# Picking both sides' indices of a head in three VectorE steps of 512 columns in place of six of 256, with the row buffers moved to the front of the memory

## The chip, the core and the metric

The kernel runs on one core of a Trainium2 chip. The metric is the device time of one launch in microseconds (us), lower is better. TensorE (PE) multiplies matrices, VectorE (DVE) and ScalarE (ACT) work on 128 partitions at a time, GpSimd (POOL) issues the indirect gathers, SyncE (SP) the plain loads. The engines run beside each other and meet at semaphores; each takes its own instructions in the order of the program.

## What is computed

Two layers of a decoder trunk on 256 tokens of width 1024. Each layer has a mixing part (norm, one input projection, pooling and attention, output projection) and a feed-forward part that looks up experts by product keys:

```
q = (xc @ w_q).reshape(TOKEN_CHUNK, PEER_HEADS, 2, PEER_HALF)
s = einsum('thpd,pkd->thpk', q, sub_keys)           # 8 heads, 2 sides, 128 keys
sv, si = top_k(s, 16)                               # per head and side
cand = sv[:, :, 0, :, None] + sv[:, :, 1, None, :]  # 16 x 16 sums
cand_id = si[:, :, 0, :, None] * 128 + si[:, :, 1, None, :]
cv, ci = top_k(cand.reshape(..., 256), 16)
eid = take_along_axis(cand_id.reshape(..., 256), ci)
g = softmax(cv)
y = einsum('thk,thkd->td', g * gelu(einsum('thkd,td->thk', u[eid], xc)), v[eid])
```

So every token reads 8 x 16 = 128 rows of `u` and of `v` per layer, from tables of 16384 rows of 1024 float32. That is the bulk of what the kernel moves.

## The kernel before

**Windows and ticks.** The tokens are cut into two tiles of 128, a token per partition, and a window is one tile in one layer: `windows` = 4, in the order layer 0 tile 0, layer 0 tile 1, layer 1 tile 0, layer 1 tile 1. A window has 64 ticks of two expert rows each, 128 rows in all. A row is one gather by POOL (L1365): for each of the 128 tokens one line of `uv`, u and v side by side, 8 KB per partition and 1 MB in all, into one of seven buffers of `ring`. The last four rows are gathered in halves (L1371, L1376).

**A row's way.** VectorE's `dot` (L1201) multiplies the u half with the token, 1024 columns, and adds it up. ScalarE makes the row's weight of it (L887 to L895). Then the v half is added to the token in one of two ways: either ScalarE spreads the weight over a diagonal (L905) and TensorE multiplies diagonal and row into the two `ybank` sums (L686, four instructions a row), or VectorE adds it itself (`weighted`, L1214). `rows_on_tensor` says which: in ticks that lie in the set `shared`, row 0 goes to VectorE, otherwise both go to TensorE. When the sum has taken a row, its buffer is free and POOL gathers the row seven places on.

**The mix of the next window** and its picking run between the rows. `streamed` walks over all ticks, and on each engine it issues the rows of a tick and whatever of the mix generators (`vector_mix`, `tensor_mix`, `scalar_mix`) has come due; each `yield` in those names the tick at which the next piece is due. So every engine's order is fixed, and a piece of mix on VectorE stands between two dots. `first_heads`, `later_heads` and `last_heads` give the ticks of the eight heads' three stages.

**The picking of a head** on VectorE, in `vector_mix`: `key_search` finds the 16 best keys of each side (`sv` their scores, `si` their indices), `all_sums` forms the 256 sums, `sum_search` finds the 16 best (`cv`, and `ci` their places), `places` splits a place into its two indices `cabf` (side 0 and side 1). `pick_side(a, lo, n, hot)` then looks up `si` at these for one side, in three steps, each of which waits for the one before (`settle`): L981 compares the index with 0 to 15 and so writes a one-hot table, L984 multiplies it with the side's key indices `sif`, L987 adds up each line of it into `picked`. For 16 experts the table has 16 x 16 = 256 columns; it is laid over the head's `score`, which is no longer wanted. `experts` (L992, L1000) makes the expert's number of the two, for which POOL waits (`expert_ready`), and `weigh_heads` (L1029, L1031) finishes the softmax. In the general case side 0 is picked half a tick before side 1, so that one dot lies between them.

Head 0 of the first window is taken in two parts, since nothing can be gathered before it: `first_experts` publishes the very best expert (L1015), then seven more from the 8 x 8 best sums, with `pick_side` on 64 columns; eight more follow behind the first dot, with 128 columns.

**Start of the rows.** The gathers of rows 3 to 6 use ring buffers that held weights of window 1 until then; POOL waits until `next_keys_values` on TensorE (L495, L505) has read them.

**Loads.** SP loads the weights in chunks of 1 MB: the first into `ring` buffers, twelve into `held`, all others into the two slots of `wring`.

Of the kernel before, what the change touches and what calls it, by code (L numbers as in the profile page):

```python
# [13 lines left out]
P = 128  # L14
S = 256
NT = S // P
D = 1024
# [116 lines left out]
def build(nc, consts, chunks, uv, x, side, rows, w_pool, pool_scale, out):  # L134
# [3 lines left out]
    with ExitStack() as ctx:  # L138
# [15 lines left out]
        first_gainT = cst[:, C_GAIN:C_DIST].rearrange("p (n k) -> p n k", n=2)  # L154
        later_gainT = beside[:, KEYS:].rearrange("p (n k) -> p n k", n=2)
        wpool = sb("wpool", [P, NG, GOUT])
        held = sb("held", [P, HELD, CHUNK])
        wring = sb("wring", [P, W_SLOTS, CHUNK])
        carry = sb("carry", [P, NG * REACH])
# [18 lines left out]
        cv = sb("cv", [P, TOPK])  # L178
        ci = sb("ci", [P, TOPK], U32)
        cab = sb("cab", [P, 2, TOPK], U32)  # L180
        best = sb("best", [P, 2])
        cabf = sb("cabf", [P, 2, TOPK])
        picked = sb("picked", [P, 2, TOPK])
        cmax = sb("cmax", [P, 1])
# [1 line left out]
        prob = sb("prob", [P, HK])  # L186
        expert = sb("expert", [P, HK], U32)

        last_halves = sb("last_halves", [P, 2, HALVED], U32)
        half_ssq = sb("half_ssq", [P, 1])  # L190

        buf1 = sb("buf1", [P, 2 * D])
        gates = buf1[:, :]
# [7 lines left out]
        merged = buf2[:, D:2 * D]  # L201
        mergedT = merged.rearrange("p (k n) -> p k n", n=P)

        ring = sb("ring", [P, RING, 2 * D])

        next_hT_made = ring[:, 0, D:2 * D].rearrange("p (k n) -> p k n", n=P)
        next_hT = buf1[:, D:2 * D].rearrange("p (k n) -> p k n", n=P)
        dots = sb("dots", [P, COLS])
        half_p = sb("half_p", [P, COLS])
        sq = sb("sq", [P, 2])  # L210
# [698 lines left out]
        def step(ins):  # L909
            ins.then_inc(dve_step, 1)  # L910
            steps[0] += 1
# [11 lines left out]
        def vector_mix(dve, w):  # L923
# [49 lines left out]
                    maximum()  # L973
                    places(TOPK, 4)

            def pick_side(a, lo, n, hot):


                best = hot.shape[2]
                these = slice(lo, lo + n)  # L980
                step(dve.tensor_tensor(hot, cabf[:, a, these].unsqueeze(2).to_broadcast([P, n, best]),  # L981
                                       iota16[:, 0:best].unsqueeze(1).to_broadcast([P, n, best]), ALU.is_equal))
                settle(dve)
                step(dve.tensor_tensor(hot, hot, sif[:, a, 0:best].unsqueeze(1).to_broadcast([P, n, best]),  # L984
                                       ALU.mult))
                settle(dve)
                step(dve.tensor_reduce(picked[:, a, these], hot, AX.X, ALU.add))  # L987
                settle(dve)

            def experts(h, lo, n):  # L990
# [9 lines left out]
                dve.tensor_scalar(expert[:, h * TOPK + lo:h * TOPK + lo + n], picked[:, 0, these],  # L1000
                                  float(layer * EXPERTS), None, ALU.add).then_inc(expert_ready, 1)

            def one_hot(h):
                return score[:, 2 * h:2 * h + 2, :].rearrange("p a (k i) -> p (a k) i", i=TOPK)

            def first_experts():


                for r in range(2):
                    dve.wait_ge(*read(w, f"score0{'ab'[r]}"))  # L1010
                    key_search(0, (r,))

                step(dve.tensor_copy(best[:, :], si[:, :, 0]))
                settle(dve)
                dve.scalar_tensor_tensor(out=expert[:, 0:1], in0=best[:, 0:1], scalar=float(NK),  # L1015
                                         in1=best[:, 1:2], op0=ALU.mult, op1=ALU.add).then_inc(expert_ready, 1)
                sums = tmp[:, 0:64]
                square = sums.rearrange("p (i j) -> p i j", i=8)
                all_sums(square, 8)
                search(lambda r: cv[:, :], lambda r: ci[:, :], lambda r: sums, range(1), (0,))  # L1020
                places(8, 3)
                for a in range(2):
                    pick_side(a, 0, 8, square)
                experts(0, 1, 7)

            def weigh_heads(h):
# [123 lines left out]
            if w == 0:  # L1150
                yield head_tick(w, 0, 0)
                first_experts()
                key_search(0, eights=(8,))
                yield head_tick(w, 0, 1)
                sum_search(0, 0)
                sum_search(0, 8)
                weigh_heads(0)
                yield head_tick(w, 0, 2)
                for a in range(2):
                    pick_side(a, 8, 8, tmp[:, 0:P].rearrange("p (k i) -> p k i", i=TOPK))  # L1160
                experts(0, 8, 8)
            for h in range(0 if w else 1, PH):
                yield head_tick(w, h, 0) - 0.5
                dve.wait_ge(*read(w, f"score{h}"))
                key_search(h)
                yield head_tick(w, h, 0)
                key_search(h, eights=(8,))
                yield head_tick(w, h, 1) - 0.5
                sum_search(h, 0)
                yield head_tick(w, h, 1)  # L1170
                sum_search(h, 8)
                yield head_tick(w, h, 2) - 0.5
                pick_side(0, 0, TOPK, one_hot(h))
                yield head_tick(w, h, 2)
                pick_side(1, 0, TOPK, one_hot(h))
                experts(h, 0, TOPK)
                weigh_heads(h)

# [104 lines left out]
        def last_scalar(act):  # L1283
            act.activation(warm[:, 2:3], gelu_bias[:, :], ACT.Sqrt)
            act.wait_ge(x_final, 2 * windows - 1)
            act.activation(gates[:, BANK:D], x_of(1)[:, BANK:D], ACT.Square,
                           accum_out=stat[:, 1, 0:1]).then_inc(ssq_done, 1)
            act.wait_ge(pe_summed, all_summed)
            act.activation(gates[:, 0:BANK], ybank[0][:, :], ACT.Square, accum_out=half_ssq[:, 0:1]
                           ).then_inc(ssq_done, 1)  # L1290
            act.wait_ge(rinv_done, 2 * windows + 2)
            act.activation(stat[:, 1, 2:3], stat[:, 1, 1:2], ACT.Sqrt).then_inc(root_done, 1)
            act.wait_ge(root_done, 2 * windows + 2)
            act.wait_ge(gained, 3)
            act.activation(normed(1)[:, BANK:D], normed(1)[:, BANK:D], ACT.Copy,
                           scale=stat[:, 1, 2:3]).then_inc(normed_a, 1)

        def last_vector(dve):
            dve.wait_ge(x_final, 2 * windows - 1)
            dve.tensor_tensor(normed(1)[:, BANK:D], x_of(1)[:, BANK:D],  # L1300
                              filled_bank(dve, windows, "final1")[:, :], ALU.mult).then_inc(gained, 1)
            mean = stat[:, 1, 1:2]
            dve.wait_ge(ssq_done, 2 * windows + 2)
            step(dve.tensor_scalar(mean, stat[:, 1, 0:1], 1.0 / D, EPS, ALU.mult, ALU.add))
            settle(dve)
            dve.wait_ge(ssq_done, 2 * windows + 3)
            step(dve.scalar_tensor_tensor(out=mean, in0=half_ssq[:, 0:1], scalar=1.0 / D, in1=mean,
                                          op0=ALU.mult, op1=ALU.add))
            settle(dve)
            dve.reciprocal(mean, mean).then_inc(rinv_done, 1)  # L1310
            dve.wait_ge(root_done, 2 * windows + 2)
            dve.scalar_tensor_tensor(out=normed(1)[:, 0:BANK], in0=ybank[0][:, :], scalar=stat[:, 1, 2:3],
                                     in1=last_gain, op0=ALU.mult, op1=ALU.mult).then_inc(normed_v, 1)
# [153 lines left out]
```

## Time and profile before

| | before |
|---|---|
| time, median of 3 runs (lowest to highest) | 1557.82 us (1556.91 to 1558.1) |
| time of the profiled execution | 1556.39 us |
| its span, first to last instruction | 1554.6 us |
| PE busy | 1274.8 us (82%) |
| DVE busy, instructions | 1152.1 us (74%), 2697 |
| ACT busy | 912.9 us (59%) |
| POOL busy | 652.4 us (42%) |
| bytes moved, mean rate | 643.51 MB, 414 GB/s |
| of them by the gathers' queue | 536.90 MB |
| chain that ended last: DMA / PE / DVE / ACT / issue | 42 / 22 / 22 / 6 / 5% |
| POOL's gathers idle before: waiting for TensorE's sums (L686) | 525.6 us |
| the same, waiting for VectorE's sums (L1214) | 212.8 us |

The profile is of one execution; its time is to be read beside its span, and the 1.8 us between them lie around the program. A busy share is an average over stages with different limits. The idle time of POOL is mostly a gather that waits for a buffer, which does not by itself say that the transfer came too late: the gathers are issued ahead of the DMA engines, and where these have a row in hand all the time, an earlier issue moves nothing.

### The profile page before, as it was taken

To read this page: it belongs to the slowest core of one execution; us is meant where nothing else is said; L and a number is where in the kernel's file an instruction comes from. 1 tells how busy PE (TensorE), PEld (TensorE's weight loads), DVE (VectorE), ACT (ScalarE), POOL (GpSimd) and SP (SyncE) were. 2 spreads that over 40 slices of the span, in tenths; PEclk is the share of its full clock that TensorE was granted. 3 is DMA by queue.
4 is the path that set the end of the run, shared out by engine and by line. 5 is a ranking of instruction groups with operands and counts; after the bars stand their busy time and mean duration, and the time that the engine had idled before them with its cause. 6 is when DMAs were issued, how large, how long until landed. Compare 5 with 4: busy or idle time off the path is not lost.

```text
span 1554.6 us, 18817 instructions
## 1 busy us (share of the span) xinstructions
PE 1274.8 (82%) x5582; PEld 784.7 (50%) x5582; DVE 1152.1 (74%) x2697; ACT 912.9 (59%) x3311; POOL 652.4 (42%) x520
## 2 busy tenths in 40 slices
PE   8999898876898688856688878797878887777876
PEld 8986576543454466633355545574445532222322
DVE  2159999777888869635789886986778787777555
ACT  2226556457666546434676664565676666666676
POOL 0014444454535333323554342334654454554554
PEclk9999899997999899986899999999999999999999
DMA  9989999999999999999999999999999999999998
GB/s 393 390 337 402 390 413 426 427 426 427 423 409 403 420 426 426 426 426 425 426 425 421 391 412 426 427 426 426 427 426 394 413 426 426 427 427 427 427 416 326
DMA packets 90318, 643.51 MB, mean 414 GB/s; under 512 B 10040, under 2 KB 10600, under 8 KB 12904
## 3 DMA queue, kind: packets, MB, share of 16 engines
q0 software_dynamic: 74304, 536.90, 82.9%
q1 hardware_dynamic: 15588, 105.18, 16.3%
q8 instruction: 44, 0.72, 0.2%
q14 instruction: 58, 0.48, 0.1%
q10 hardware_dynamic: 324, 0.23, 0.0%
HBM read 641.23 MB, written 1.05 MB: 413 GB/s over the span
## 4 chain that ended last, share of the span: by engine, by line
DMA 42%; PE 22%; DVE 22%; ACT 6%; issue 5%; POOL 2%; DVEq 0%; POOLq 0%; ACTq 0%
DMA ring<-in_uv,expert 41%; PE ybank L686 12%; DVE ring L1201 8%; PE bank L483 6%; DVE xs L1214 3%; PE bank L629 2%; POOL ring L1365 2%; ACT diag L905 1%; DMA wring<-in_chunks 1%; ACT wgt L895 1%; DVE si L940 1%; ACT th L893 1%; DVE buf L934 1%; DVE buf L984 1%; DVE picked L987 1%
## 5 line engine op out<-in xcount | busy, mean ns | idle before, releaser
L1365 POOL DMA_INDIRECT ring<-in_uv,expert x508 | 642.4, 1265 | 884.6 <-PE ybank L686 525.6
L686 PE MATMUL ybank<-ring,diag 128*128 128x512 f32 x1528 | 782.2, 647 | 255.4 <-ACT diag L905 254.2
L1201 DVE SCALAR_TENSOR_TENSOR ring<-ring,tok 128x1024 f32<-128x1024 f32 x512 | 624.2, 1224 | 286.6 <-DMA ring<-in_uv,expert 280.7
L686 PEld LDWEIGHTS ybank<-ring,diag 128*128 128x128 f32 x1528 | 280.7, 199 | 646.6 <-ACT diag L905 412.8
L887 ACT ACTIVATE sq<-dots 128x1 f32<-128x1 f32 x512 | 102.5, 200 | 490.7 <-DVE ring L1201 489.5
L895 ACT ACTIVATE wgt<-th,half_p 128x1 f32<-128x1 f32 x512 | 198.1, 387 | 17.1
L483 PEld LDWEIGHTS bank<-hT,wring 128*128 128x128 f32 x1536 | 188.6, 201 | 34.7 <-issue 33.2
L483 PE MATMUL bank<-hT,wring 128*128 128x128 f32 x1536 | 189.2, 284 | 7.9 <-DMA wring<-in_chunks 7.6
L1214 DVE SCALAR_TENSOR_TENSOR xs<-ring,wgt,xs 128x1024 f32<-128x1024 f32 x128 | 164.2, 1283 | 5.8 <-ACT wgt L895 4.3
L905 ACT ACTIVATE diag<-cst,wgt 128x128 f32<-128x128 f32 x384 | 154.2, 402 | 18.6 <-PE ybank L686 6.3
L893 ACT ACTIVATE th<-arg,dots 128x1 f32<-128x1 f32 x512 | 150.8, 295 | 16.6
L888 ACT ACTIVATE half_p<-dots,prob 128x1 f32<-128x1 f32 x512 | 142.9, 279 | 0.2
L890 ACT ACTIVATE arg<-sq,gelu_bias 128x1 f32<-128x1 f32 x512 | 142.9, 279 | 0.0
L483 PEld LDWEIGHTS bank<-hT,held 128*128 128x128 f32 x736 | 89.3, 198 | 12.4 <-issue 12.4
L483 PE MATMUL bank<-hT,held 128*128 128x128 f32 x736 | 88.8, 280 | 0.0
L629 PE MATMUL bank<-held,buf 128*128 128x256 f32 x256 | 58.6, 384 | 0.0
L629 PEld LDWEIGHTS bank<-held,buf 128*128 128x128 f32 x256 | 49.5, 194 | 13.4 <-issue 7.1
L483 PE MATMUL bank<-hT,ring 128*128 128x128 f32 x448 | 51.8, 278 | 0.0
L483 PEld LDWEIGHTS bank<-hT,ring 128*128 128x128 f32 x448 | 51.0, 194 | 0.7 <-DMA ring<-in_chunks 0.4
L696 ACT ACTIVATE buf<-bank 128x256 f32<-128x256 f32 (+2 forms) x65 | 28.4, 444 | 32.0 <-PE bank L483 29.3
L1201 DVE DVE_READ_ACCUMULATOR ring<-ring,tok 128x1 f32 x512 | 42.0, 82 | 0.0
L940 DVE FIND_INDEX8 si<-sv,buf 128x8 uint32<-128x128 f32 x128 | 35.0, 285 | 0.0
(143 smaller groups left out, 798.5 us busy)
## 6 DMA issues: line engine op xcount, KB each, us to landing
wring<-in_chunks SPq DMA_DIRECT2D x52, 1024.0 KB
held<-in_chunks SPq DMA_DIRECT2D x24, 1024.0 KB, 26.1
ring<-in_chunks SPq DMA_DIRECT2D x20, 1024.0 KB, 11.2
ring<-in_uv,expert POOLq DMA_INDIRECT x508
xs<-in_x SPq DMA_DIRECT2D x2, 512.0 KB, 4.6
wpool<-in_w_pool SPq DMA_DIRECT2D x2, 512.0 KB, 12.9
trunk_out<-buf SPq DMA_DIRECT2D x4, 256.0 KB, 4.7
ring<-in_pool_scale SPq DMA_DIRECT2D x1, 512.0 KB, 13.6
```

The lines of the kernel that those rows point to most:

```text
L483: ins = pe.matmul(b[:, m * CW + lo:m * CW + lo + P], wt[k][:, lo:lo + P], hT[:, k, :], start=(k == 0), stop=(k == KC - 1))
L629: ins = pe.matmul(b[:, 0:CW], mergedT[:, k, :], wt[k][:, :], start=(k == 0), stop=(k == KC - 1))
L686: ins = pe.matmul(ybank[m][:, :], diag[:, nth % DIAGS, :], ring[:, (2 * t + r) % RING, D + m * BANK:D + (m + 1) * BANK], start=(nth == ten ...
L887: act_stepped(act.activation(sq[:, r:r + 1], dots[:, c:c + 1], ACT.Square))
L888: act.activation(half_p[:, c:c + 1], dots[:, c:c + 1], ACT.Copy, scale=prob[:, 2 * n + r:2 * n + r + 1])
L890: act_stepped(act.activation(arg[:, r:r + 1], sq[:, r:r + 1], ACT.Identity, scale=0.044715 * GELU_C, bias=gelu_bias[:, 0:1]))
L893: act_stepped(act.activation(th[:, r:r + 1], arg[:, r:r + 1], ACT.Tanh, scale=dots[:, c:c + 1]))
L895: ins = act.activation(wgt[:, c:c + 1], th[:, r:r + 1], ACT.Identity, scale=half_p[:, c:c + 1], bias=half_p[:, c:c + 1])
L905: act.activation(diag[:, nth % DIAGS, :], ident, ACT.Copy, scale=wgt[:, c:c + 1]).then_inc(diag_done, 1)
L1201: dve.scalar_tensor_tensor(out=ring[:, g % RING, 0:D], in0=ring[:, g % RING, 0:D], scalar=1.0, in1=tok[:, :], op0=ALU.mult, op1=ALU.mult, ...
L1214: dve.scalar_tensor_tensor(out=total, in0=ring[:, (2 * t + r) % RING, D:2 * D], scalar=wgt[:, c:c + 1], in1=total, op0=ALU.mult, op1=ALU.a ...
L1365: pool.indirect_dma_start(ring[:, g % RING, :], None, uv, bass.IndirectOffsetOnAxis(ap=expert[:, at:at + 1], axis=0)).then_inc(row_landed[ ...
```

## The change

`pick_side` is replaced by `mark` and `pick`, which work on both sides at once: 2 x 16 x 16 = 512 columns in place of two times 256 (2 x 8 x 8 and 2 x 8 x 16 for the two parts of head 0). The table has a buffer of its own, `both`, of 2 KB per partition. In the general case the mark stands where the picking of side 0 stood, one dot ahead of the rest. `ring` is allocated ahead of `held`: it begins at byte 26176 of a partition in place of 168192 (26176 = 102 x 256 + 64, 168192 = 657 x 256); `held` began at 26176 and begins at 83520 now. `best`, `half_ssq` and `last_halves` are laid into `picked`, `ssum` and `si`.

```diff
+        ring = sb("ring", [P, RING, 2 * D])
         held = sb("held", [P, HELD, CHUNK])
...
-        best = sb("best", [P, 2])
...
-        last_halves = sb("last_halves", [P, 2, HALVED], U32)
-        half_ssq = sb("half_ssq", [P, 1])
+        last_halves = si[:, :, 0:HALVED]
+        half_ssq = ssum[:, 0:1]
...
-        ring = sb("ring", [P, RING, 2 * D])
...
+        both = sb("both", [P, 2 * TOPK * TOPK])
...
-            def pick_side(a, lo, n, hot):
-                best = hot.shape[2]
-                these = slice(lo, lo + n)
-                step(dve.tensor_tensor(hot, cabf[:, a, these].unsqueeze(2).to_broadcast([P, n, best]),
-                                       iota16[:, 0:best].unsqueeze(1).to_broadcast([P, n, best]), ALU.is_equal))
+            def mark(lo, n, hot):
+                best = hot.shape[3]
+                step(dve.tensor_tensor(hot, cabf[:, :, lo:lo + n].unsqueeze(3).to_broadcast([P, 2, n, best]),
+                                       iota16[:, 0:best].unsqueeze(1).unsqueeze(1).to_broadcast([P, 2, n, best]),
+                                       ALU.is_equal))
                 settle(dve)
-                step(dve.tensor_tensor(hot, hot, sif[:, a, 0:best].unsqueeze(1).to_broadcast([P, n, best]),
-                                       ALU.mult))
+
+            def pick(lo, n, hot):
+                best = hot.shape[3]
+                step(dve.tensor_tensor(hot, hot, sif[:, :, 0:best].unsqueeze(2).to_broadcast([P, 2, n, best]), ALU.mult))
                 settle(dve)
-                step(dve.tensor_reduce(picked[:, a, these], hot, AX.X, ALU.add))
+                step(dve.tensor_reduce(picked[:, :, lo:lo + n], hot, AX.X, ALU.add))
                 settle(dve)
...
-                for a in range(2):
-                    pick_side(a, 0, 8, square)
+                dve.wait_ge(expert_ready, 1)
+                hot = both[:, 0:128].rearrange("p (a k i) -> p a k i", a=2, i=8)
+                mark(0, 8, hot)
+                pick(0, 8, hot)
                 experts(0, 1, 7)
...
                 yield head_tick(w, h, 2) - 0.5
-                pick_side(0, 0, TOPK, one_hot(h))
+                hot = both[:, :].rearrange("p (a k i) -> p a k i", a=2, i=TOPK)
+                mark(0, TOPK, hot)
                 yield head_tick(w, h, 2)
-                pick_side(1, 0, TOPK, one_hot(h))
+                pick(0, TOPK, hot)
                 experts(h, 0, TOPK)
                 weigh_heads(h)
```

What this does to VectorE's order, in the picking of head 1 in the first window (L1201, afterwards L1203, is a dot). Before:

```order
L981 TENSOR_TENSOR buf<-cabf,cst 128x256
L984 TENSOR_TENSOR buf<-buf,sif 128x256
L987 TENSOR_REDUCE picked<-buf 128x16
L1201 SCALAR_TENSOR_TENSOR ring,dots<-ring,tok 128x1024
L981 TENSOR_TENSOR buf<-cabf,cst 128x256
L984 TENSOR_TENSOR buf<-buf,sif 128x256
L987 TENSOR_REDUCE picked<-buf 128x16
L992 SCALAR_TENSOR_TENSOR picked<-picked 128x16
```

and now:

```order
L979 TENSOR_TENSOR both<-cabf,cst 128x512
L1203 SCALAR_TENSOR_TENSOR ring,dots<-ring,tok 128x1024
L986 TENSOR_TENSOR both<-both,sif 128x512
L988 TENSOR_REDUCE picked<-both 128x32
L993 SCALAR_TENSOR_TENSOR picked<-picked 128x16
```

One step stands ahead of the dot where three stood, and two of 512 columns behind it where three of 256 stood. In `first_experts`, ahead of any dot, before:

```order
L958 CAST cabf<-cab 128x2x8
L981 TENSOR_TENSOR buf<-cabf,cst 128x64
L984 TENSOR_TENSOR buf<-buf,sif 128x64
L987 TENSOR_REDUCE picked<-buf 128x8
L981 TENSOR_TENSOR buf<-cabf,cst 128x64
L984 TENSOR_TENSOR buf<-buf,sif 128x64
L987 TENSOR_REDUCE picked<-buf 128x8
L992 SCALAR_TENSOR_TENSOR picked<-picked 128x7
```

and now:

```order
L958 CAST cabf<-cab 128x2x8
L979 TENSOR_TENSOR both<-cabf,cst 128x128
L986 TENSOR_TENSOR both<-both,sif 128x128
L988 TENSOR_REDUCE picked<-both 128x2x8
L993 SCALAR_TENSOR_TENSOR picked<-picked 128x7
```

Three steps of 128 columns stand in place of six of 64. The instructions of TensorE, ScalarE, POOL and SP and their order stay as they are.

## Rows read from the trace of the kernel before

**Rows 1.** The page, DMA row.

```profile
DMA packets 90318, 643.51 MB, mean 414 GB/s; under 512 B 10040, under 2 KB 10600, under 8 KB 12904
```

**Rows 2.** Stretches: us, busy us of each engine, granted PE clock, DMA share, GB/s.

```profile
54.00:64.00 10.00, 10.00 (x93) 9.88 (x91) 0.00 (x0) 1.70 (x5) 0.00 (x0) 1.00 1.01 425
88.00:94.00 6.00, 6.00 (x32) 5.16 (x30) 0.46 (x2) 1.14 (x4) 0.00 (x0) 1.00 1.01 425
100.00:130.00 30.00, 26.93 (x152) 20.78 (x152) 28.18 (x101) 13.04 (x42) 12.29 (x12) 1.00 0.86 318
130.00:160.00 30.00, 27.49 (x165) 20.08 (x163) 28.58 (x74) 20.57 (x79) 14.04 (x12) 1.00 1.01 425
160.00:200.00 40.00, 35.19 (x183) 24.87 (x184) 38.69 (x115) 20.36 (x77) 17.28 (x12) 0.87 0.98 381
200.00:460.00 260.00, 215.70 (x1000) 137.97 (x999) 218.40 (x488) 164.29 (x605) 120.52 (x95) 0.93 1.01 425
460.00:475.00 15.00, 15.00 (x77) 9.98 (x76) 13.48 (x29) 9.17 (x37) 5.97 (x6) 1.00 0.88 333
860.00:870.00 10.00, 10.00 (x42) 5.84 (x41) 8.69 (x16) 6.12 (x25) 5.97 (x6) 1.00 0.81 289
1190.00:1202.00 12.00, 12.00 (x51) 7.70 (x51) 10.45 (x26) 6.79 (x26) 4.09 (x5) 0.94 0.88 349
```

**Rows 3.** Groups of VectorE by form: busy us, mean ns, idle before and its releaser.

```profile
L1201 DVE SCALAR_TENSOR_TENSOR ring<-ring,tok 128x1024 f32<-128x1024 f32 x512 | 624.2, 1224 | 286.6 <-DMA ring<-in_uv,expert 280.7 <-issue 1.4
...
L984 DVE TENSOR_TENSOR buf<-buf,sif 128x256 f32<-128x256 f32 x62 | 26.4, 425 | 2.1
L981 DVE TENSOR_TENSOR buf<-cabf,cst 128x256 f32<-128x256 f32 x62 | 26.1, 421 | 0.0
L987 DVE TENSOR_REDUCE picked<-buf 128x16 f32<-128x256 f32 x62 | 26.0, 420 | 2.1
...
L1138 DVE TENSOR_TENSOR buf<-buf 128x512 f32<-128x512 f32 x8 | 5.5, 692 | 0.8
...
L1070 DVE SCALAR_TENSOR_TENSOR buf<-cst,bank 128x256 f32<-128x256 f32 x16 | 6.0, 417 | 0.2
```

**Rows 4.** Timeline of VectorE, 130 to 142 us: start, duration.

```profile
130.09 0.42 DVE L981 TENSOR_TENSOR buf<-cabf,cst 128x256 f32<-128x256 f32 x1
130.55 0.43 DVE L984 TENSOR_TENSOR buf<-buf,sif 128x256 f32<-128x256 f32 x1
...
141.04 1.28 DVE L1214 SCALAR_TENSOR_TENSOR xs<-ring,wgt,xs 128x1024 f32<-128x1024 f32 x1 [0.24 <-ACT wgt L895]
```

**Rows 5.** Timeline of POOL's gathers, with the idle time before and its releaser.

```profile
107.96 0.94 POOL L1365 DMA_INDIRECT ring<-in_uv,expert  x1 [0.83 <-PE bank L495]
...
189.12 1.68 POOL L1365 DMA_INDIRECT ring<-in_uv,expert  x1 [5.72 <-DVE xs L1214]
```

**Rows 6.** Timeline of TensorE, 103 to 126 us.

```profile
111.06 7.07 PE L505 MATMUL bank<-ring,buf 128*128 128x256 f32 x32
117.97 7.03 PE L686 MATMUL ybank<-ring,diag 128*128 128x512 f32 x16
```

**Rows 7.** Pieces of the chain that ended last: start, us, what.

```profile
103.02 0.23 DVE buf L984
...
156.46 0.43 DVE buf L984
...
178.33 0.42 DVE buf L984
...
1403.67 0.43 DVE buf L984
```

**Rows 8.** Timeline of TensorE, 852 to 866 us.

```profile
858.70 7.13 PE L686 MATMUL ybank<-ring,diag 128*128 128x512 f32 x16
```

**Rows 9.** Timeline of VectorE, dots within a picking at 841 and 1179 us.

```profile
841.02 1.22 DVE L1201 SCALAR_TENSOR_TENSOR ring<-ring,tok 128x1024 f32<-128x1024 f32 x1
...
1179.04 1.23 DVE L1201 SCALAR_TENSOR_TENSOR ring<-ring,tok 128x1024 f32<-128x1024 f32 x1 [0.70 <-DMA ring<-in_uv,expert]
```

More of the change, by code:

```diff
@@ L1001, in experts @@
                                   float(layer * EXPERTS), None, ALU.add).then_inc(expert_ready, 1)
-            def one_hot(h):
-                return score[:, 2 * h:2 * h + 2, :].rearrange("p a (k i) -> p (a k) i", i=TOPK)
             def first_experts():
@@ L1011, in first_experts @@
                     key_search(0, (r,))
-                step(dve.tensor_copy(best[:, :], si[:, :, 0]))
+                step(dve.tensor_copy(picked[:, :, 0], si[:, :, 0]))
                 settle(dve)
-                dve.scalar_tensor_tensor(out=expert[:, 0:1], in0=best[:, 0:1], scalar=float(NK),
-                                         in1=best[:, 1:2], op0=ALU.mult, op1=ALU.add).then_inc(expert_ready, 1)
+                dve.scalar_tensor_tensor(out=expert[:, 0:1], in0=picked[:, 0, 0:1], scalar=float(NK),
+                                         in1=picked[:, 1, 0:1], op0=ALU.mult, op1=ALU.add).then_inc(expert_ready, 1)
                 sums = tmp[:, 0:64]
@@ L1158, in vector_mix @@
                 yield head_tick(w, 0, 2)
-                for a in range(2):
-                    pick_side(a, 8, 8, tmp[:, 0:P].rearrange("p (k i) -> p k i", i=TOPK))
+                hot = both[:, 0:2 * P].rearrange("p (a k i) -> p a k i", a=2, i=TOPK)
+                mark(8, 8, hot)
+                pick(8, 8, hot)
                 experts(0, 8, 8)
@@ L1288, in last_scalar @@
             act.wait_ge(pe_summed, all_summed)
-            act.activation(gates[:, 0:BANK], ybank[0][:, :], ACT.Square, accum_out=half_ssq[:, 0:1]
+            act.activation(gates[:, 0:BANK], ybank[0][:, :], ACT.Square, accum_out=half_ssq
                            ).then_inc(ssq_done, 1)
@@ L1306, in last_vector @@
             dve.wait_ge(ssq_done, 2 * windows + 3)
-            step(dve.scalar_tensor_tensor(out=mean, in0=half_ssq[:, 0:1], scalar=1.0 / D, in1=mean,
+            step(dve.scalar_tensor_tensor(out=mean, in0=half_ssq, scalar=1.0 / D, in1=mean,
                                           op0=ALU.mult, op1=ALU.add))
```

## The prediction, made before the changed kernel had run

> **What bounds the kernel now.** First the page's DMA row [rows 1]: 643.51 MB cross the DMA engines in the span of 1554.6 us, a mean of 414 GB/s. Then a table of stretches [rows 2], whose last column is what the DMA moved. It is to be read against a ceiling: from 200 to 460 us, and in every stretch of which nothing is said below, it is 425 to 427 GB/s at a DMA share of 1.01, whatever the other engines do. At 427 GB/s the bytes alone need 643.51 / 0.427 = 1507 us, so the kernel is bound by its transfers, and all that can be won is the 48 us in which the pipe is not full. A stretch loses its length times (427 minus its rate) / 427: 7.7 us in 100 to 130, 0.1 in 130 to 160, 4.3 in 160 to 200, 3.3 in 460 to 475, 3.2 in 860 to 870, 2.2 in 1190 to 1202. The other 27 us lie mostly before 100 and after 1490 us, where no head is picked, the rest in crumbs. The change acts on VectorE, so the question for each lost stretch is whether VectorE's picking stands in the way of the next gather there.
>
> **What the change saves on VectorE.** One head has six picking steps of 256 columns: compare (L981), multiply (L984), add up (L987), for each side. They take 421, 425 and 420 ns [rows 3], and 0.46 us pass from the start of one to the start of the next (130.09 to 130.55 [rows 4]): 6 x 0.457 = 2.74 us. Afterwards there are three steps of 512 columns. No step of that form ran before: compare and multiply now read operands with three levels. The lower bound is the plain 128x512 step, 692 ns [rows 3]; the upper bound is two steps of 256 in one, 0.91 us, with which nothing is saved. I take 692 ns plus the same 0.035 us to the next start, 0.725 us, because steps of 256 with two-level operands cost what a plain one does (421 and 425 against 417 for L1070 [rows 3]), so levels have cost nothing so far. Three steps are 2.18 us: **0.57 us less per head**. The two small parts of head 0 have the same fixed cost per step to save, three times some 0.19 us, and come to 0.57 each too. All in all 33 x 0.57 = 18.8 us. The halves are also cut otherwise: the mark before a dot takes 0.73 us where 1.37 stood, and the second block, pick with `experts` and `weigh_heads`, has two steps of 0.725 where it had three of 0.457, **0.08 us more** than before.
>
> **What of it reaches the end.** A saving counts only where the pipe has a gap that it shortens.
> *100 to 130 us:* `first_experts` publishes seven experts 0.57 us earlier, and the gathers of rows 1 and 2 follow at once. But those of rows 3 to 6 wait for `next_keys_values` on TensorE (L495, L505 [rows 5]), whose last part runs from 111.06 us and is followed without a gap by sixteen products of L686, four rows, until 125.0 [rows 6]. They don't move, nor do the gathers that wait for them. Two gathers start earlier, and the pipe is empty behind them for as long. Gain 0.
> *130 to 160 us:* the pipe is full at 425 GB/s. At 141.04 VectorE waits for ScalarE's weight of a row that has only just landed [rows 4], so what head 0 and head 1 have saved by then is spent in waiting. Gain 0.
> *160 to 200 us:* VectorE is busy 38.69 of 40 us [rows 2], and gathers wait for L1214, the weighted rows on VectorE, one of them 5.72 us [rows 5]. The chain of waits runs through VectorE without a break, with the picking of head 2 (a multiply at 156.46) and of head 3 (at 178.33) in it [rows 7]. Both are 0.57 shorter: **1.14 us** of the 4.3 lost here. The next head's picking, at 199 us, has a full pipe behind it.
> *The dips at 460, 860 and 1190 us* are TensorE's: 15.00 of 15, 10.00 of 10, 12.00 of 12 us busy [rows 2]; at 860 it works through sixteen row products from 858.70 on [rows 8], late behind other work. What can start such a pile sooner is a dot on VectorE that runs sooner. But the dot between the halves of the picking ahead of it (841.02 [rows 9]) comes 2.5 us after the one before, the pace at which rows land (1.05 MB at 427 GB/s are 2.46 us); at 1179.04 VectorE even waits 0.70 us there for its row [rows 9]. So the shorter mark only waits longer, and what reaches the pile is the second block, 0.08 us longer: three times, 0.2 us at most, of which I count 0.1.
>
> **The rest of the edit.** `ring` moves from byte 168192 of a partition to 26176: it starts 64 bytes past a multiple of 256, not on one. The nearest rows: from 54 to 64 us the loads go into `held`, which lies 64 bytes past a multiple of 256 before the change, and from 88 to 94 into `ring`, which lies on one: 425 and 425 GB/s [rows 2]. I take 0. The Trainium skill speaks against the change here: "DMA: Bandwidth & Descriptors", section "How a descriptor splits into AXI transactions", has a descriptor that doesn't start 256B-aligned pay for the bytes below its start. By it a row's 256 beats would be 258, and the kernel would be slower by 0.8% of its gathers; the two rates above don't bear that out. The wait for `expert_ready` added to `first_experts` is for VectorE's own instruction, done long before: 0. `best`, `half_ssq` and `last_halves`, laid into other tensors, change no instruction: 0. Nothing moves on TensorE, ScalarE, POOL or SP.
>
> **The sum**, against the profiled execution's 1556.39 us: -1.14 + 0.1 = -1.0, so 1555.4. The median of the three runs is 1557.82, 1.4 above the profiled one, so the forecast for the median is 1556.8. About 0.2%, 3.1 us, is what a measurement can tell from no change; this is inside it.
>
> **The rivals.**
> *A: the chain is right as it stands.* It holds a side's multiply 30 times, from 103.02 to 1403.67 us [rows 7]. If each such side gives its 0.285 us to the end, 8.6 us go: 1549.2. For it: from 99 to 196 us the chain is nearly all VectorE. Against it: most of the 30 lie where the pipe is full, and a chain names one path where two are equally late. It decides if the gaps at 100 to 130 and the three dips shrink too. Half of it would give 1553.5.
> *B: the row buffers' new place costs transfer time.* If the start 64 bytes past a multiple of 256 costs each gather one part in 128, the 508 gathers take 508 x 2.46 x 0.0078 = 9.8 us longer, all of it on the pipe: 1557.82 + 9.8 = 1567.6, slower. It decides once the full stretches fall from 427 to about 425; at 426.7 it has taken back the whole forecast. Against it is the load of `held`.
> *C: the steps are not shorter.* If the three-level operands cost, a step takes 0.91 us and the change does nothing: 1557.8. At 1.2 us a head pays 3 x 1.2 - 2.74 = 0.9 us more; heads 2 and 3 in their gap and one block at each of three dips are 5 x 0.9 = 4.5 us: 1562.3.
>
> **How the numbers follow.** The forecast (from 2.5 us faster to 1 slower) gets 0.62, A in full or half 0.22, B 0.06, C 0.10, half of it near 0.91 us and so without effect. Faster by over 0.2% are A and the forecast's far edge: 0.24. Slower are B, the dear half of C, and 0.01 for gathers that fall badly: 0.12. Within: 0.64. The low end, 1552.0, takes in the half of A; the high end, 1560.5, the steps between 0.91 and 1.1 us. A in full, B and the dear end of C stay outside, not quite 2 in 10.
>
> **What would show it.** In the profile after: L979, L986 and L988 at 0.68 to 0.70 us for 512 columns; VectorE's busy time down by 17 to 19 us; the full stretches still at 425 to 427 GB/s; the loss in 160 to 200 us down by about 1 of its 4.3 us; those of 100 to 130, 460, 860 and 1190 us as before within 0.3; VectorE's wait for landed rows, 280.7 us in all [rows 3], up by most of the saving. I am wrong by A if the dips at the window ends shrink by over half a microsecond each, by B if the full stretches fall by 2 GB/s, by C if a step takes over 0.85 us.

## The result, and the profile after

The changed kernel takes 1573.37 us (median of four), beside 1557.37 us for the kernel before on the same chip: ratio 1.0100, 95% interval 1.0085 to 1.0115. It is **slower by 1%, about 16 us**, where 1 us faster was forecast. Three of its runs took 1571.37, 1572.02 and 1574.72 us; the fourth, a slow one of 3435.15 us, stands in that median (1572.02 us without it) and not in the ratio.

| | before | after |
|---|---|---|
| profiled execution | 1556.39 us | 1572.02 us |
| span | 1554.6 us | 1570.2 us |
| DVE busy, instructions | 1152.1 us, 2697 | 1136.2 us, 2598 |
| PE / ACT / POOL busy | 1274.8 / 912.9 / 652.4 us | 1282.2 / 912.8 / 657.3 us |
| bytes moved, mean rate | 643.51 MB, 414 GB/s | 643.51 MB, 410 GB/s |
| VectorE waiting for landed rows | 280.7 us | 317.5 us |

From the page of the changed kernel: busy times, the rate in 40 slices of the span, the DMA row that answers to [rows 1], and the shares of the chain.

```profile
PE 1282.2 (82%) x5582; PEld 787.2 (50%) x5582; DVE 1136.2 (72%) x2598; ACT 912.8 (58%) x3311; POOL 657.3 (42%) x520
...
GB/s 394 399 335 407 399 420 420 421 421 421 409 390 418 421 421 419 420 421 417 422 402 414 381 421 420 419 420 421 415 421 407 391 421 422 421 422 421 422 409 327
DMA packets 90317, 643.51 MB, mean 410 GB/s; under 512 B 10040, under 2 KB 10600, under 8 KB 12904
...
DMA 46%; PE 25%; DVE 16%; ACT 6%; issue 5%; POOL 2%; DVEq 0%; POOLq 0%; ACTq 0%
```

VectorE does less than before and the bytes are the same, but no slice is above 422 GB/s. The same row of the kernel before, for comparison:

```profile
GB/s 393 390 337 402 390 413 426 427 426 427 423 409 403 420 426 426 426 426 425 426 425 421 391 412 426 427 426 426 427 426 394 413 426 426 427 427 427 427 416 326
```

Most slices that don't hold a gap were at 425 to 427 and are at 419 to 422. That alone is about the size of the result: the gathers move 536.90 MB, and 536.90 / 0.421 less 536.90 / 0.427 is 17.9 us. The table of stretches of the changed kernel answers to [rows 2] (same columns: us, busy us of PE, PEld, DVE, ACT, POOL, granted clock, DMA share, GB/s), with two stretches more:

```profile
54.00:64.00 10.00, 10.00 (x98) 9.88 (x98) 0.00 (x0) 1.88 (x6) 0.00 (x0) 1.00 1.01 425
64.00:84.00 20.00, 20.00 (x161) 19.01 (x158) 4.47 (x7) 3.74 (x5) 0.00 (x0) 1.00 1.01 419
88.00:94.00 6.00, 5.70 (x31) 4.80 (x30) 1.13 (x3) 1.66 (x6) 0.00 (x0) 1.00 1.01 422
100.00:130.00 30.00, 27.77 (x160) 21.62 (x158) 28.13 (x95) 14.31 (x47) 14.21 (x13) 1.00 0.90 338
130.00:160.00 30.00, 27.66 (x153) 19.31 (x152) 28.28 (x70) 19.65 (x74) 12.82 (x12) 0.97 1.01 421
160.00:200.00 40.00, 36.34 (x188) 25.62 (x187) 38.77 (x111) 22.78 (x87) 17.14 (x13) 0.89 0.99 398
200.00:460.00 260.00, 214.87 (x987) 137.41 (x986) 211.87 (x462) 161.36 (x591) 123.69 (x94) 0.92 1.01 419
...
1240.00:1480.00 240.00, 192.80 (x458) 74.27 (x457) 173.34 (x423) 158.77 (x588) 126.66 (x98) 1.00 1.01 419
```

The DMA share is 1.01 wherever the rate is 419 to 421: the engines are as busy as before and move less in the same time. Wherever the pipe is full the changed kernel loses, and where it has its early gaps (100 to 130 us, 160 to 200 us) it moves more than before, 338 against 318 and 398 against 381.

The steps by form, on VectorE of the changed kernel (columns as in [rows 3]), and the second block of a head at 130 us, which answers to [rows 4]:

```profile
L1203 DVE SCALAR_TENSOR_TENSOR ring<-ring,tok 128x1024 f32<-128x1024 f32 x512 | 624.5, 1224 | 322.2 <-DMA ring<-in_uv,expert 317.5
...
L979 DVE TENSOR_TENSOR both<-cabf,cst 128x512 f32<-128x512 f32 x31 | 21.3, 688 | 0.0
L986 DVE TENSOR_TENSOR both<-both,sif 128x512 f32<-128x512 f32 x31 | 21.3, 686 | 0.0
L988 DVE TENSOR_REDUCE picked<-both 128x32 f32<-128x512 f32 x31 | 21.3, 686 | 1.1
```

```profile
130.43 0.68 DVE L986 TENSOR_TENSOR both<-both,sif 128x512 f32<-128x512 f32 x1
131.15 0.69 DVE L988 TENSOR_REDUCE picked<-both 128x32 f32<-128x512 f32 x1
131.87 0.17 DVE L993 SCALAR_TENSOR_TENSOR picked<-picked 128x16 f32<-128x16 f32 x1
```

A step of 512 columns takes 686 to 688 ns and the next starts 0.72 us after it, as forecast. So the picking did what it should, and something else cost some 20 us.

### The profile page after: what moved, and what is told of

It reads as the page before. It is cut to its first block, busy times and chain, and to the rows that moved or that the text cites. A ratio compares the mean times of both kernels' runs of the same rounds, so it can differ in the third digit from the quotient of the medians.

```text
span 1570.2 us, 18719 instructions
## 1 busy us (share of the span) xinstructions
PE 1282.2 (82%) x5582; PEld 787.2 (50%) x5582; DVE 1136.2 (72%) x2598; ACT 912.8 (58%) x3311; POOL 657.3 (42%) x520
## 2 busy tenths in 40 slices
DMA packets 90317, 643.51 MB, mean 410 GB/s; under 512 B 10040, under 2 KB 10600, under 8 KB 12904
## 3 DMA queue, kind: packets, MB, share of 16 engines
q0 software_dynamic: 74304, 536.90, 82.9%
## 4 chain that ended last, share of the span: by engine, by line
DMA 46%; PE 25%; DVE 16%; ACT 6%; issue 5%; POOL 2%; DVEq 0%; POOLq 0%; ACTq 0%
DMA ring<-in_uv,expert 44%; PE ybank L686 12%; PE bank L483 8%; DVE ring L1203 6%; DVE xs L1216 2%; POOL ring L1367 2%; DMA wring<-in_chunks 2%; PE bank L629 1%; ACT wgt L895 1%; ACT diag L905 1%; ACT th L893 1%; PE bank L618 1%; PE bank L463 1%; DVE picked L988 1%; ACT arg L890 1%
## 5 line engine op out<-in xcount | busy, mean ns | idle before, releaser
L686 PE MATMUL ybank<-ring,diag 128*128 128x512 f32 x1528 | 790.3, 653 | 263.4 <-ACT diag L905 262.1
L1203 DVE SCALAR_TENSOR_TENSOR ring<-ring,tok 128x1024 f32<-128x1024 f32 x512 | 624.5, 1224 | 322.2 <-DMA ring<-in_uv,expert 317.5
L1203 DVE DVE_READ_ACCUMULATOR ring<-ring,tok 128x1 f32 x512 | 41.9, 82 | 0.0
```

The costliest lines, as they stand in the source:

```text
L686: ins = pe.matmul(ybank[m][:, :], diag[:, nth % DIAGS, :], ring[:, (2 * t + r) % RING, D + m * BANK:D + (m + 1) * BANK], start=(nth == ten ...
L1203: dve.scalar_tensor_tensor(out=ring[:, g % RING, 0:D], in0=ring[:, g % RING, 0:D], scalar=1.0, in1=tok[:, :], op0=ALU.mult, op1=ALU.mult, ...
```

## The experiments

Three theories stood at the start. **Alignment**: transfers into rows that start off a multiple of 256 bytes run slower (rival B, dearer than priced). **Place**: the front of the memory is slower for the gathers than the back. **Order**: the gathers fall worse with three steps. Every ratio is to the kernel before on the same chip; its medians were 1556.67 us (e1 to e4), 1556.07 us (e5 to e8) and 1558.35 us (e9 to e12).

**e1: the changed kernel, `ring` at the front but on a multiple of 256.** `cv` and `cab`, 192 bytes, go ahead of `ring`, which begins at 26368 = 103 x 256. `held` and `wring` move by the same 192 bytes and so come onto a multiple of 256 too; what that is worth by itself is e11's question.

```diff
+        cv = sb("cv", [P, TOPK])
+        cab = sb("cab", [P, 2, TOPK], U32)
         ring = sb("ring", [P, RING, 2 * D])
...
-        cv = sb("cv", [P, TOPK])
...
-        cab = sb("cab", [P, 2, TOPK], U32)
```

> The changed kernel with 192 bytes of small tensors (cv, cab) laid ahead of ring: ring stays at the front but starts at 26368, a multiple of 256 (held and wring start on one too). Alignment theory: the full stretches are back at 425 to 427 GB/s and the time is about 1555 to 1557 us, some 16 us below the changed kernel. Place theory (the front of the memory is slower for the DMA's writes): full stretches at 417 to 421 GB/s, 1571 to 1574 us. Picking theory (VectorE's new order makes it slower): 1571 to 1574 us too.

Measured: 1552.04 us, ratio 0.9972 (0.9962 to 0.9983). From its stretches:

```profile
64.00:84.00 20.00, 20.00 (x159) 19.01 (x156) 4.47 (x7) 3.74 (x5) 0.00 (x0) 1.00 1.01 425
...
1240.00:1480.00 240.00, 195.19 (x446) 74.27 (x447) 172.98 (x425) 163.01 (x600) 123.36 (x98) 0.99 1.01 427
```

With 192 bytes of shift the slower kernel becomes the faster one, at the front of the memory and with three steps. Place and order fall as causes. From 1.0100 to 0.9972 it is 1.3% of 1557, 20 us. It is also 3 us below the lowest time expected, which was the first sign that the picking gives more than forecast (e4).

**e2: the kernel before, `ring` at the back but 64 bytes on.** One edit: byte 168192 becomes 168256. The small tensors behind `ring` (`dots` to `gelu_bias`), into which no DMA writes, move by the same 64 bytes.

```diff
+        pad = sb("pad", [P, 16])
         ring = sb("ring", [P, RING, 2 * D])
```

> The kernel before with 64 bytes of padding ahead of ring: it starts at 168256, 64 bytes past a multiple of 256, still at the back. Alignment theory: full stretches at 417 to 421 GB/s in place of 425 to 427, and about 1557 + 1507 x 0.012 = 1575 us. Place and picking theories: no change, 1557 us.

Measured: 1575.47 us, ratio 1.0124 (1.0106 to 1.0142).

```profile
200.00:460.00 260.00, 214.46 (x978) 137.28 (x978) 214.84 (x478) 161.37 (x591) 120.17 (x94) 0.92 1.01 419
...
1240.00:1480.00 240.00, 193.23 (x465) 75.15 (x464) 176.09 (x439) 158.44 (x585) 122.15 (x97) 1.00 1.01 417
```

The cost appears whole, with no instruction changed. That is the shortest demonstration of the cause. The small tensors are not it: in e9 below they move by 896 bytes, and the ratio is 1.0008.

**e3: the kernel before with `ring` moved as in the change**, to 26176, six steps kept.

```diff
+        ring = sb("ring", [P, RING, 2 * D])
         held = sb("held", [P, HELD, CHUNK])
...
-        ring = sb("ring", [P, RING, 2 * D])
```

> The kernel before, its six picking steps unchanged, with ring allocated ahead of held as in the change (26176, 64 bytes past a multiple of 256). Alignment and place theories: about 1573 to 1575 us, the changed kernel's time and perhaps 1 to 2 more, since the picking saves that. Picking theory: 1557 us.

Measured: 1575.55 us, ratio 1.0132 (1.0113 to 1.0151); 418 GB/s from 200 to 460 us and 419 from 1240 to 1480. Nothing tells it from e2: front and back cost the same. The changed kernel's ratio stands 0.3% below it, with intervals that just touch, which points to the picking giving something even where the transfers are slow.

**e4: the changed kernel's picking with `ring` at the back on a multiple of 256** (167936; `held` at 26176 as before).

```diff
-        ring = sb("ring", [P, RING, 2 * D])
...
-        srec = sb("srec", [P, HEADS])
...
-        cab = sb("cab", [P, 2, TOPK], U32)
...
+        ring = sb("ring", [P, RING, 2 * D])
+        srec = sb("srec", [P, HEADS])
+        cab = sb("cab", [P, 2, TOPK], U32)
```

> The picking change alone: three steps of 512 columns, ring at the back on a multiple of 256 (167936). Alignment and place theories: the forecast of the picking part holds, 1555 to 1557 us. Picking theory: 1571 to 1574 us.

Measured: 1552.98 us, ratio 0.9981 (0.9971 to 0.9990).

```profile
64.00:84.00 20.00, 20.00 (x160) 19.04 (x157) 4.47 (x7) 3.77 (x6) 0.00 (x0) 1.00 1.01 420
...
100.00:130.00 30.00, 28.08 (x163) 21.93 (x162) 28.43 (x95) 14.44 (x48) 15.23 (x13) 1.00 0.90 343
...
160.00:200.00 40.00, 35.18 (x183) 24.40 (x181) 38.69 (x113) 23.35 (x89) 17.32 (x13) 0.91 0.98 398
...
1240.00:1480.00 240.00, 193.84 (x445) 73.15 (x444) 173.12 (x426) 162.71 (x601) 122.92 (x98) 1.00 1.01 427
```

This is the picking, with `ring` on the boundary at the back as before: 3.0 us faster (1.6 to 4.5), against 1.0 forecast. It closes the account of the change: e2's 19.3 us less 3.0 are 16.3, and 15.6 were measured. By lost time of the two profiled executions it is 1.6 us in 160 to 200 us (40 x 46/427 less 40 x 29/427), where 1.14 was forecast, and 1.8 us in 100 to 130 us (30 x 109/427 less 30 x 84/427), where 0 was. POOL's timeline shows why. The kernel before (start, duration, and in brackets the idle time before and its releaser):

```profile
101.47 1.07 POOL L1365 DMA_INDIRECT ring<-in_uv,expert  x1 [101.02 <-DVE expert L1015]
104.95 0.94 POOL L1365 DMA_INDIRECT ring<-in_uv,expert  x1 [2.40 <-DVE expert L1000]
...
129.30 1.67 POOL L1365 DMA_INDIRECT ring<-in_uv,expert  x1 [2.75 <-DVE xs L1214]
```

and e4, the same three gathers:

```profile
100.83 1.07 POOL L1367 DMA_INDIRECT ring<-in_uv,expert  x1 [100.38 <-DVE expert L1013]
103.73 0.94 POOL L1367 DMA_INDIRECT ring<-in_uv,expert  x1 [1.83 <-DVE expert L1001]
...
127.60 1.68 POOL L1367 DMA_INDIRECT ring<-in_uv,expert  x1 [1.60 <-DVE xs L1216]
```

The first comes 0.64 us earlier, ahead of any picking. The second comes 1.22 us earlier, 0.58 beyond that: the first part of head 0. The third waits for a row that VectorE adds itself, which stands behind both parts of head 0 in VectorE's order: 1.70 us earlier, 1.06 beyond the start, both parts.

The early start is no work of the change. The same three gathers in e7 (below), with six steps as in the kernel before:

```profile
100.69 1.07 POOL L1366 DMA_INDIRECT ring<-in_uv,expert  x1 [100.24 <-DVE expert L1016]
104.16 0.94 POOL L1366 DMA_INDIRECT ring<-in_uv,expert  x1 [2.40 <-DVE expert L1001]
...
128.51 1.68 POOL L1366 DMA_INDIRECT ring<-in_uv,expert  x1 [2.74 <-DVE xs L1215]
```

Over all fourteen profiles the first gather starts between 100.69 and 101.52 us, early and late with either picking. Counted from it, the third of these comes 27.82 to 27.84 us later wherever head 0 and the later heads have six steps, and 26.77 us later in e1, e4, e5 and e12 (27.00 in the changed kernel). So some 1.1 of the 1.8 us at 100 to 130 us is the picking's, and the rest is put down to the start. The 1.6 us at 160 to 200 us is one profile against one, too: with six steps for the later heads and `ring` on the boundary the stretch reads 381, 377 and 389 GB/s (before, e5, e11), with three 390, 398 and 406 (e1, e4, e12). The means are 1.5 us apart.

**e5 and e6: the saving divided.** Both have e4's layout; e5 takes only head 0's two parts in three steps, e6 only the other 31 heads.

```diff
-                hot = both[:, :].rearrange("p (a k i) -> p a k i", a=2, i=TOPK)
-                mark(0, TOPK, hot)
+                pick_side(0, 0, TOPK, one_hot(h))
                 yield head_tick(w, h, 2)
-                pick(0, TOPK, hot)
+                pick_side(1, 0, TOPK, one_hot(h))
```

(of e5; e6 puts `pick_side` back for the two parts of head 0 in the same way.)

> Memory laid out as in e4 (ring on a multiple of 256), but only the two parts of head 0 are picked in three steps; the 31 other pickings have six steps of 256. The picking change alone measured 3.0 us faster (e4). If that comes from the first gathers starting earlier (100 to 130 us), this one gives 1 to 2 us of it: 1555 to 1556 beside 1556.7. If it comes from the later heads, as the prediction had it, nothing: 1556.7, and the loss in 160 to 200 us stays at 4.3 us.

> The other half: head 0 of the first window keeps its six steps, the 31 other pickings have three. By the prediction's own sum it gives all of what can be had, 1.0 us: 1555.7 beside 1556.7, with 160 to 200 us losing 3.2 in place of 4.3. If the chain of waits was right also for the dips at 460, 860 and 1190 us, 2 us or more: 1554.7 or less, and these dips are shorter by 0.3 us or more each.

Measured: e5 1554.10 us, 0.9989 (0.9978 to 1.0000); e6 1555.12 us, 0.9992 (0.9980 to 1.0004). First e5, then e6:

```profile
100.00:130.00 30.00, 28.08 (x163) 21.93 (x162) 28.36 (x97) 14.57 (x48) 15.34 (x13) 1.00 0.91 338
...
160.00:200.00 40.00, 35.63 (x186) 24.88 (x185) 38.69 (x113) 21.61 (x82) 17.50 (x12) 0.89 0.98 377
```

```profile
100.00:130.00 30.00, 26.92 (x145) 20.47 (x145) 28.00 (x101) 13.05 (x42) 12.53 (x12) 0.97 0.88 326
130.00:160.00 30.00, 28.93 (x168) 21.53 (x167) 28.72 (x70) 21.02 (x79) 13.49 (x12) 0.97 0.99 400
160.00:200.00 40.00, 35.64 (x187) 25.14 (x187) 38.82 (x111) 22.05 (x83) 18.15 (x13) 0.91 1.01 413
```

The profiles divide it as e4 suggests: head 0's parts fill 100 to 130 us and leave 160 to 200 as it was, the later heads do the reverse, though in e6 part of the gap only moved ahead of 160 us (and its 326 GB/s at 100 to 130 us are those of e7, e9 and e11, 325, which have six steps and an early start). The two ratios give 1.7 and 1.2 us, which add up to e4's 3.0, but each interval reaches to no change, so their sizes are not settled. The dips at 460, 860 and 1190 us are shorter in e6 (341, 343 and 394 GB/s), as its text had it for the chain of waits; e11 shows below that such differences come with six steps as well.

**e7 and e8: other distances.** The kernel before with 128 bytes ahead of `ring` (168320), and with 32 (168224).

```diff
+        pad = sb("pad", [P, 32])
         ring = sb("ring", [P, RING, 2 * D])
```

```diff
+        pad = sb("pad", [P, 8])
         ring = sb("ring", [P, RING, 2 * D])
```

> The kernel before with ring 128 bytes past a multiple of 256. If any start off a multiple of 256 costs, the same: 1575 us, full stretches at 417 to 420 GB/s. If the cost goes by the distance from the boundary (the bytes below the start), more than at 64: 1590 us. If a multiple of 128 is enough: 1557 us.

> The kernel before with ring 32 bytes past a multiple of 256. Any start off a multiple of 256 costs the same: 1575 us. By the distance: about 1566 us. If a start that is no multiple of 64 costs more: over 1580 us.

Measured: 128 bytes 1572.49 us, 1.0107 (1.0086 to 1.0128); 32 bytes 1577.54 us, 1.0136 (1.0113 to 1.0158). Their rates from 1240 to 1480 us, first e7, then e8:

```profile
1240.00:1480.00 240.00, 192.21 (x456) 73.77 (x455) 176.47 (x441) 159.20 (x587) 125.26 (x98) 1.00 1.01 420
```

```profile
1240.00:1480.00 240.00, 192.55 (x465) 74.97 (x463) 176.04 (x439) 158.81 (x586) 123.66 (x96) 1.00 1.01 418
```

The cost does not grow with the distance: 32, 64 and 128 bytes give 1.36, 1.24 and 1.07%, with intervals that overlap. Of the starts tried, what matters is to be off the multiple of 256.

**e9 and e10: buffers partly on it.** The kernel before with a wider row pitch in `ring`: by 128 bytes, so that four of the seven buffers start on a multiple of 256 and three 128 past it, and by 64 bytes, so that two of seven do.

```diff
-        ring = sb("ring", [P, RING, 2 * D])
+        ring_wide = sb("ring", [P, RING, 2 * D + 32])
+        ring = ring_wide[:, :, 0:2 * D]
```

(in e10 `2 * D + 16`).

> The kernel before with 128 unused bytes behind each row buffer: four of the seven buffers start on a multiple of 256, three 128 bytes past one, in turn. If every gather into a buffer off the boundary costs for itself, 3/7 of the 15.8 us of e7: 6.8 us, 1563, full stretches at 423 to 424 GB/s. If gathers on the boundary beside it absorb the cost (as the chunk loads into wring, off the boundary, did at 425 to 427 GB/s beside gathers on it), nothing: 1556, full stretches at 426 to 427.

> The kernel before with 64 unused bytes behind each row buffer: two of seven start on a multiple of 256, the others 64, 128 or 192 past one. Each for itself: 5/7 of 18.8 us, 13.4 us, 1570, full stretches at about 421 GB/s. Absorbed by those on the boundary: between 1556 and 1565, the more of the cost the fewer of them; with four of seven (e9) less than half of this.

Measured: e9 1559.94 us, 1.0008 (0.9994 to 1.0021); e10 1566.99 us, 1.0064 (1.0042 to 1.0086). First e9, then e10:

```profile
1240.00:1480.00 240.00, 194.67 (x466) 76.29 (x465) 174.47 (x438) 159.76 (x591) 119.82 (x97) 0.99 1.01 423
```

```profile
1240.00:1480.00 240.00, 193.45 (x469) 75.30 (x468) 174.28 (x438) 160.24 (x592) 120.22 (x98) 1.00 1.01 424
```

Five of seven off the boundary cost half of what seven do. Three of seven, alternating with four on it, cost less than their share of some 0.5%: the interval ends at 0.21%. The profiled execution of e9, at 1563.21 us the slowest of its ten, shows 423 GB/s, but e11, with every buffer on the boundary, shows 425 in that stretch, so this settles little. The cost is not simply one price per misaligned row; what makes up for it between neighbours is not shown.

**e11: the kernel before with everything on multiples of 256**, `held` and `wring` too (26368 and 168448 begin `held` and `ring`).

```diff
+        pad = sb("pad", [P, 48])
         held = sb("held", [P, HELD, CHUNK])
...
+        pad2 = sb("pad2", [P, 16])
         ring = sb("ring", [P, RING, 2 * D])
```

> The kernel before with held and wring on a multiple of 256 too (ring was on one already). The stretch from 64 to 84 us, loads into held and wring alone, rises from 419 to 425 GB/s, and the time falls by 20 x 6/427 = 0.3 us and perhaps as much again where held is loaded beside the gathers: 1555.5 beside 1556.1, which the interval may not tell from nothing. Place theory, if anything is left of it: no change.

Measured: 1557.72 us, ratio 0.9994 (0.9984 to 1.0003): no change that can be told. But one stretch changes, which is the one that counts for the prediction. The kernel before, and e11:

```profile
64.00:84.00 20.00, 20.00 (x166) 19.12 (x166) 4.47 (x7) 4.33 (x6) 0.00 (x0) 1.00 1.01 419
...
1240.00:1480.00 240.00, 194.25 (x445) 73.39 (x446) 175.27 (x443) 162.91 (x599) 120.46 (x97) 1.00 1.01 427
```

```profile
64.00:84.00 20.00, 20.00 (x163) 19.06 (x160) 4.47 (x7) 3.96 (x6) 0.00 (x0) 1.00 1.01 426
```

From 64 to 84 us the loads go into `held` and `wring` alone. 64 bytes off they run at 419 GB/s, on the boundary at 426. All fourteen profiles agree: 419 to 421 in the eleven with `held` and `wring` off it, 425, 426 and 426 in e1, e11 and e12. The price is 20 x 7/427 = 0.3 us, too little to be timed.

**e12: the changed kernel's picking with everything on multiples of 256**, `ring` at the back (167936), `held` at 26368.

```diff
-        ring = sb("ring", [P, RING, 2 * D])
+        cv = sb("cv", [P, TOPK])
+        cab = sb("cab", [P, 2, TOPK], U32)
         held = sb("held", [P, HELD, CHUNK])
...
-        srec = sb("srec", [P, HEADS])
...
-        cv = sb("cv", [P, TOPK])
...
-        cab = sb("cab", [P, 2, TOPK], U32)
-        cabf = sb("cabf", [P, 2, TOPK])
...
+        ring = sb("ring", [P, RING, 2 * D])
+        srec = sb("srec", [P, HEADS])
+        cabf = sb("cabf", [P, 2, TOPK])
```

> The picking change with ring at the back, and ring, held and wring all on multiples of 256. It is e1 with the row buffers at the back: if the place in the memory is nothing, the same as e1, 1552 us, 0.3% under the kernel before; if the back is better or worse, apart by more than a microsecond.

Measured: 1551.80 us, ratio 0.9963 (0.9950 to 0.9977), span 1549.4 us.

```profile
64.00:84.00 20.00, 20.00 (x166) 19.08 (x163) 4.47 (x7) 4.17 (x6) 0.00 (x0) 1.00 1.01 426
...
160.00:200.00 40.00, 34.53 (x186) 24.06 (x184) 38.72 (x114) 23.07 (x88) 17.73 (x13) 0.96 1.00 406
...
1240.00:1480.00 240.00, 194.04 (x441) 73.58 (x442) 172.08 (x419) 162.73 (x599) 120.86 (x97) 0.99 1.01 427
```

It beats both kernels: by its ratio 5.8 us under the one before, some 21 us (1.4%) under the changed one. Against e1 (0.9962 to 0.9983), which has it all on multiples of 256 at the front, the intervals overlap.

The runs that bear on the cause, in one table (ratio to before):

| | `ring` on a multiple of 256 | `ring` 64 bytes past it |
|---|---|---|
| six steps, back | 1 (before) | 1.0124 (e2) |
| six steps, front | not tried | 1.0132 (e3) |
| three steps, front | 0.9972 (e1) | 1.0100 (the change) |
| three steps, back | 0.9981 (e4), 0.9963 (e12) | not tried |

Down a column the picking gives 0.2 to 0.4%; across a row the 64 bytes cost 1.2 to 1.3%. (In e1 and e12 `held` and `wring` are on the boundary too; e11 puts that at 0.0006, and at 0.0016 at most.)

## Why the prediction was wrong

**The step that failed** is the one on the rest of the edit, "I take 0" for `ring` 64 bytes past a multiple of 256. It costs 19 to 20 us (e2: 1.24% of 1557, 19 us; the change against e1: 20 us, with the other loads' buffers in it). Rival B named the mechanism and its sign, and the chance of 0.06 was far too low.

**Why it was taken at 0.** The evidence was two rates, 425 GB/s into `held` from 54 to 64 us and 425 into `ring` from 88 to 94. The first of them misled: it is the first 10 us of the loads into `held`, where the eleven profiles with `held` off the boundary read 423 to 426 and the three with it on 426 to 428. The next 20 us of the same loads read 419 in the kernel before. That row was in the trace of before, and 419 is the rate at which the gathers run after the change; it also goes against the prediction's sentence that every stretch of which it says nothing runs at 425 to 427. One more stretch would have turned the forecast. The other half of the control was sound: from 88 to 94 us the loads into `ring` read 425 to 429 in the seven profiles with all of `ring` on the boundary and 419 to 422 in the five with all of it off.

**Size of B.** It was priced at one part in 128, 9.8 us. Measured, full slices fell from 427 to 421, 1.4%, and the time rose by 19 to 20 us, twice that. The check named in the text, "if the full stretches fall by 2 GB/s", was the right one; they fell by 6 to 8. The Trainium skill, "DMA: Bandwidth & Descriptors", section "How a descriptor splits into AXI transactions", spoke against the change and had the sign, but it tells of what a misaligned start makes a transfer read. By it, as an estimate, a row at 32, 64 and 128 bytes would be 257, 258 and 260 beats for 256, a cost that grows fourfold. Here only the place written to was moved, and e8, e2 and e7 show no growth (1.36, 1.24 and 1.07%). The measurement decides: that arithmetic does not give the size here.

**What the change saves on VectorE** was right. 0.686 to 0.688 us a step where 0.692 was taken, 0.72 us from one to the next where 0.725 was; rival C is out. Busy time fell by 15.9 us, below the 17 to 19 forecast: that range took the time from start to start for busy time. By the rows it is 31 x (2 x 1.266 - 2.06) = 14.6 us for the 31 whole heads; the rest lies in head 0's parts and crumbs.

**What of it reaches the end** was right in kind and low in size: 3.0 us (e4) against 1.0. The term for 160 to 200 us, 1.14, came out at about 1.5 (1.6 in e4). The term for 100 to 130 us, "gain 0", failed. Its argument, that the gathers of rows 3 to 6 wait for TensorE, holds (they move only with the start), but it stopped at row 6. The gather at 129.30 us is released by L1214 on VectorE, and what VectorE saves on head 0 reaches it whole: 1.06 us, of which the pipe got back about 1.1. The dips at 460, 860 and 1190 us can't be read for this: they lose 8.7 us in the kernel before and 5.5 us in e11 (376, 294 and 405 GB/s in the three stretches), with the same six steps and only addresses moved, so the forecast of 0.1 us there is neither shown nor refuted.

**Rival A** in full, 8.6 us, is out: with the transfers undisturbed the gain is 3.0 us (e4; 4.5 at most) or, with `held` and `wring` on the boundary too, 4.4 and 5.8 us (e1, e12; 7.8 at most). Its half, 4.3 us, lies inside e4's interval, and one of its two conditions, that the gap at 100 to 130 us shrinks, did hold. Where in the transfers' gaps a saving lands was better told by the chain than I granted.

**The wait of VectorE** for landed rows rose by 36.8 us in the changed kernel, by 19.3 in e4 (280.7 to 300.0). The second is the saving, which only waits longer, as forecast. The slower rows alone, in e2, give 20.5 (301.2), so the first is about both together.

**What stays open.** What in the path of a transfer makes a row that starts off the boundary dearer, whatever the distance, and why such rows between others that start on it cost little (e9), was not isolated. Nor was it found why some plain loads hardly show the cost: those into `held` from 54 to 64 us, and the first ones into `ring`, which from 9 to 17 us run at 428 GB/s in the changed kernel and at 427 in the kernel before. The first gather's start, 100.69 to 101.52 us, varies by up to 0.8 us between profiles. It depends on no picking, and the cause was not found; how much of it is in the times compared here is not known.

## What to carry to other kernels

Where transfers bound a kernel, print the byte address of every buffer that is written by DMA and keep it on a multiple of 256, as far as these rows of 8 KB tell: allocating small tensors behind the large ones, or 192 bytes ahead of them, was worth 1.3% here, three to seven times what the rewritten computation gave. When an edit to an allocation rides along with an edit to the work, time each alone. And before a cost is set to zero by a row of the trace, take the longest stretch in which nothing else runs, and not its first few microseconds.

## What the runs showed of the hardware

- 8 KB per partition, gathered from HBM into SBUF rows that start 32, 64 or 128 bytes past a multiple of 256, move at 417 to 420 GB/s (1240 to 1480 us of the changed kernel, e2, e3, e7, e8) where rows on it move at 427 (before, e1, e4, e5, e6, e12; 425 in e11), with the DMA share at 1.01 in both. Plain 1 MB loads show the same from 64 to 84 us, 419 to 421 against 425 and 426, but hardly from 54 to 64 us, 423 to 426 against 426 to 428.
- The distance makes no difference that the intervals show, nor does the place of the buffers in the memory: byte 26368 or 167936 on the boundary (e1, e12), 26176 or 168256 off it (e3, e2).
- The cost isn't additive: seven of seven buffers off the boundary cost 1.24%, five of seven 0.64%, three of seven 0.08% (-0.06 to 0.21; e2, e10, e9).
- A VectorE step over operands with three levels (128x512, f32) takes 686 to 688 ns in the changed kernel, no more than plain ones of that size in the same profile, 678 to 699 ns (L1115, L1138).
